# Merging the input projection and the gating stage of a hybrid decoder step, with two-part fp32r products

## The chip, the cores and the metric

The kernel runs on one core of one Trainium2 chip. The metric is the device time of one execution in microseconds (us), from the core's first instruction to its last plus a little around it. Three runs of the kernel before gave 2077.75 us in the median (2077.49 to 2078.82).

## The reference, cut to what matters

The reference is one step of a decoder layer for 1024 prompt tokens and 32 sample tokens (8 sequences of 4), 1056 in all, each with 1024 features. The part in question is its beginning:

```python
h = _rmsnorm(x, p['g_mix'])
u, v, q, kc, vc, ks, vs, kw, vw, gates = _split_in(h @ p['w_in'])   # 512, 512, 512, 6 x 128, 24 columns
...
u = gelu(u); v = _layernorm(gelu(v), ln_v_g, ln_v_b)                # _gmlp_mixer
mixed = einsum('gts,ncsgd->nctgd', w_s * causal, v) + b_s           # _sgu: 8 groups, chunks of 128 tokens
a_out = u * mixed
...
merged = concat([_rmsnorm(a_out, g_a), _rmsnorm(b_out, g_b)])       # _mix_out
x = x + merged @ w_o
```

Between `a_out` and `merged` stand the compression of keys and values, the attention of the samples and the attention of the prompt; after it come cross-attention and a gated feed-forward part. Everything is float32 at the interface.

## The kernel before

**Stages.** `program` runs the stages one after another, each a block in which the five engines have their own instruction streams and which all engines leave together: `input_phase`, `gating_phase`, `compress_phase`, `sample_attention`, `prompt_attention`, `mix_output`, then cross-attention and the feed-forward part. A tensor in SBUF is either feature-major (features on the 128 partitions, tokens along the row, `K.XT`, `K.HT`, `K.FM`) or token-major (128 tokens on the partitions, `K.U`, `K.V`, `K.VT`).

**input_phase** (L153). SP loads x in three pieces of 352 tokens. ACT squares each piece (L103), TensorE sums the squares over the features with a matrix of ones (L124, eight matmuls a piece), ACT takes the root (L133), VectorE inverts it and writes h = x * gain / rms into `K.HT` (L140, L147). Only then come the products: 8 chunks of 128 output features (q, and four of the key and value parts) times 3 pieces, each of 8 fp32 matmuls of 352 columns (L265), evacuated by ACT (L238). A ring of two buffers takes the weights. From the third chunk on, one piece of the bias rows is made behind each chunk (L274, 33x8 times up to 512 columns; L243). SP's queue also carries all other loads in program order: the token-major weights `w_tm`, two gathers of two sequences each (L295: 8 pages of 128 KB a sequence, whose numbers are read from the page table into registers), the operands of the gating, and at the end the writes of the bias rows, `fm` and the old window rows (`win_old`, from DRAM to DRAM).

**gating_phase** (L313). For each of 9 tiles of 128 tokens (the last has 32) TensorE makes u, v and the rest as 8 fp32 matmuls each of 512, 512 and 280 columns, with `K.HT` as the stationary operand and the weights as the moving one (L373). ACT applies gelu (L388, L389) and the sums for the layer norm, VectorE normalises v and copies the rest out. For each pair of tiles, 8 matmuls mix v over the tokens (L362), and VectorE adds the bias and multiplies by u (L418). SP loads the weights of the compression (`w_cmp1`, 1 MB each for k and v) when the last product is done.

**compress_phase** (L456). VectorE splits rows of `K.FM` (L498); SP moves them, then gathers the second half of the sequences, loads windows and gathers the selected pages (L295); TensorE runs six rounds (L573, L567, L586, L591). PE begins only when both halves of `w_cmp1` are there.

**mix_output** (L1056). The gated part is token-major: ACT squares it (L1124), VectorE scales it (L1159), TensorE turns each tile with four transposes (L1213), VectorE takes it out (L1164). The attention part is feature-major and goes through `FeatureNorm`. The product with `w_o` is 3 pieces x 8 chunks (L1230); turns of later tiles stand between the chunks.

**The feed-forward part** already splits operands: a number is held as high (rounded to fp32r by ACT) and low (the rest, by VectorE or POOL), and a product is three fp32r matmuls, high*high, high*low and low*high (L1622, L1640; the splits in L1722, L1731, L1784 and L1591).

Of the kernel before, what the change touches and what calls it, by code (L numbers as in the profile page):

```python
# [18 lines left out]
F32R = mybir.dt.float32r  # L19
I32 = mybir.dt.int32  # L20
ALU = mybir.AluOpType
# [131 lines left out]
def input_phase(nc, K, I, O):  # L153

    S = K.sem
    hold = K.top[:, O_VT:O_VT + 2 * KD * FREE3]
    sq = [hold[:, KD * FREE3 * u:KD * FREE3 * (u + 1)].rearrange("p (c n) -> p c n", c=KD) for u in range(2)]
    L = VECS + VECW
    oh = K.top[:BUCKETS + 1, O_M:O_M + L]
    vec = K.top[:H, O_M + L:O_M + 2 * L]  # L160
    root = [K.top[:, O_M + 2 * L + FREE3 * u:O_M + 2 * L + FREE3 * (u + 1)] for u in range(2)]
    ring = K.top[:, O_FM - 2 * KD * P:O_FM].rearrange("p (u k n) -> p u k n", u=2, k=KD)
    norm = FeatureNorm(nc, K, "mix", K.XT, K.gains[:, 0, :], PIECES, sq, root, K.bank[6], adds=0)
    const_came, eps_set, ones_set = S("const_came"), S("eps_set"), S("ones_set")
    x_came = [S(f"x_came{p}") for p in range(3)]
    w_came = [S(f"fm_w{u}") for u in range(2)]
    done, taken = S("fm_product"), S("fm_taken")
    came, rows, stored, product, set_ = S("bias_came"), S("bias_rows"), S("bias_dram"), S("bias_product"), S("bias_table")
    cuts = [(x, min(x + 512, L)) for x in range(0, L, 512)]
    tiles = [(c, p) for p in range(3) for c in range(2)] + [(c, p) for c in range(2, KD) for p in range(3)]  # L170
    nth = {tile: n for n, tile in enumerate(tiles)}

    with nc.Block() as block:
        @block.sync
        def _(sp):
            def weights(c):
                if c >= 2:
                    sp.wait_ge(done, nth[c - 2, 2] + 1)
                sp.dma_start(ring[:, c % 2], I["w_fm"][c]).then_inc(w_came[c % 2], 16)

            for p, (a, b) in enumerate(PIECES):
                sp.dma_start(K.XT[:, :, a:b], I["xt"][:, :, a:b]).then_inc(x_came[p], 16)
                if p == 0:
                    sp.dma_start(K.ident[:, :], I["ident"]).then_inc(const_came, 16)
                    sp.dma_start(K.gains[:, :, :], I["gains"]).then_inc(const_came, 16)
            weights(0)
            weights(1)
            sp.dma_start(oh, I["oh_v"]).then_inc(came, 16)
            sp.wait_ge(set_, 1)
            sp.dma_start(K.table[:BUCKETS, :], I["rel_bias"]).then_inc(came, 16)  # L190
            sp.dma_start(K.page_table[:, :], I["page_table"]).then_inc(came, 16)
            w = K.big[:, O_W:O_W + KD * TMW].rearrange("p (k n) -> p k n", k=KD)
            for k in range(KD):
                sp.dma_start(w[:, k, :], I["w_tm"][k]).then_inc(K.wtm_sem, 16)
            weights(2)
            sp.wait_ge(norm.scaled, 3)
            sp.wait_ge(came, 48)
            gather(sp, K, 0, "cmp", 0, 2)
            weights(3)
            gather(sp, K, 0, "cmp", 2, 2)  # L200
            for c in range(4, KD):
                weights(c)
                if c == 5:
                    for to, of in gating_operands(K, I):
                        sp.dma_start(to, of).then_inc(K.gating_sem, 16)
# [16 lines left out]
        def _(act):  # L222
            def square(p):
                act.wait_ge(x_came[p], 16)
                for h in range(2):
                    norm.square(act, p, h)
# [1941 lines left out]
```

## Time and profile before

| | |
|---|---|
| median of three runs | 2077.75 us |
| the profiled execution, its time | 2076.87 us |
| its span, first to last instruction | 2075.0 us |
| first product of the input stage starts | 30.09 us |
| first product of the gating stage starts | 157.58 us |
| first product of the compression starts | 336.12 us |
| sample attention starts (TensorE) | 408.48 us |
| product with `w_o` runs | 732.33 to 859.53 us |

PE is TensorE's matmuls, PEld its weight loads, DVE VectorE, ACT ScalarE, POOL GpSimd, SP the engine that issues most DMAs (SPq is its issuing). An fp32 matmul has two records in the trace, an fp32r matmul has one (the views call both f32), and records overlap, since matmuls are pipelined: the pace of a stream is its length divided by its matmuls, not the mean of a record. "[x <-y]" behind a row is the idle time before it and what ended it.

### The profile page before, as it was taken

The page shows a single profiled execution, that of the slowest core. Times are in us where ns is not written, and L with a number is a line of the kernel's source. Part 1 is how long each engine was busy: PE and PEld are TensorE (multiplying, and loading weights), DVE is VectorE, ACT ScalarE, POOL GpSimd, SP SyncE. Part 2 cuts the span into 40 slices and gives each one's busy share as a digit, 9 for nine tenths or more (in the row PEclk, how much of TensorE's full clock was granted, in tenths as well). Part 3 has the DMA queues.
Part 4 walks back from the last instruction along what each step waited for, and adds up shares of the span by engine and source line. Part 5 has one row for each costly group of instructions (what it writes and reads, how often), then busy time and mean ns, then how long its engine had stood idle before and what let it go on. Part 6 is the DMA issues. An engine that isn't in the chain of part 4 may idle for free. (4 is left out here: it accounts for less than half of the span.)

```text
span 2075.0 us, 26291 instructions
## 1 busy us (share of the span) xinstructions
PE 1935.3 (93%) x10926; PEld 1532.2 (74%) x10926; DVE 849.8 (41%) x1832; ACT 504.9 (24%) x1103; POOL 221.3 (11%) x98
## 2 busy tenths in 40 slices
PE   7999998948999789899978899999999999999997
PEld 4554555725767655656666466999999999999997
DVE  3001214047787545310032123545554555455547
ACT  2112221006888721000022022201111121112112
POOL 0000000000000000000000000313331333133320
PEclk9999999968999889999999999999999999999999
DMA  5512004741112120221033400201110111011102
GB/s 216 144 36 111 1 0 130 209 140 52 52 52 85 62 81 0 108 75 41 21 122 133 171 1 1 80 26 62 61 40 22 61 62 43 20 61 62 45 21 84
DMA packets 97002, 145.12 MB, mean 70 GB/s; under 512 B 40621, under 2 KB 73453, under 8 KB 94989
## 3 DMA queue, kind: packets, MB, share of 16 engines
q1 hardware_dynamic: 92798, 140.30, 19.8%
q10 hardware_dynamic: 4088, 3.17, 0.5%
q8 instruction: 86, 1.41, 0.3%
q14 instruction: 30, 0.25, 0.0%
HBM read 132.37 MB, written 14.19 MB: 71 GB/s over the span
## 5 line engine op out<-in xcount | busy, mean ns | idle before, releaser
L1622 PE MATMUL ps<-ff_in_high,ff_weights_low 128*128 128x352 f32 x1056 | 342.6, 324 | 0.0
L1622 PE MATMUL ps<-ff_in_high,ff_weights_high 128*128 128x352 f32 x1056 | 340.2, 322 | 0.0
L1622 PE MATMUL ps<-ff_in_low,ff_weights_high 128*128 128x352 f32 x1056 | 338.0, 320 | 0.0
L1622 PEld LDWEIGHTS ps<-ff_in_high,ff_weights_high 128*128 128x128 f32 x1056 | 198.8, 188 | 0.3
L1622 PEld LDWEIGHTS ps<-ff_in_low,ff_weights_high 128*128 128x128 f32 x1056 | 198.3, 188 | 0.2
L1622 PEld LDWEIGHTS ps<-ff_in_high,ff_weights_low 128*128 128x128 f32 x1056 | 198.1, 188 | 0.0
L1826 DVE TENSOR_TENSOR x<-ps,x 128x352 f32<-128x352 f32 x216 | 113.4, 525 | 134.5 <-PE ps L1640 134.5
L373 PE MATMUL ps<-big 128*128 128x512 f32 (+3 forms) x432 | 160.4, 533 | 6.2 <-DVE top L406 6.2
L1640 PE MATMUL ps<-ff_act_high,ff_down_high 128*128 128x352 f32 (+1 forms) x496 | 158.3, 319 | 0.2
L1640 PE MATMUL ps<-ff_act_high,ff_down_low 128*128 128x352 f32 (+1 forms) x496 | 156.5, 316 | 0.0
L1640 PE MATMUL ps<-ff_act_low,ff_down_high 128*128 128x352 f32 (+1 forms) x496 | 156.5, 315 | 0.0
L1591 POOL TENSOR_TENSOR ff_weights_low<-ff_weights,ff_weights_high 128x1024 fp32r<-128x1024 f32 x44 | 106.0, 2409 | 472.1 <-ACT ff_weights_high L1722 472.1
L373 PEld LDWEIGHTS ps<-big 128*128 128x128 f32 (+1 forms) x432 | 78.6, 183 | 86.9 <-issue 79.6
L1230 PE MATMUL ps<-big 128*128 128x352 f32 x384 | 118.9, 469 | 7.5 <-DVE big L1164 5.5
L1022 ACT ACTIVATE big<-big 128x63 f32<-128x63 f32 (+8 forms) x192 | 114.3, 608 | 21.5 <-DVE big L965 21.4
L1691 PE MATMUL ps<-big 128*128 128x352 f32 x384 | 115.6, 463 | 1.3 <-PEq L1432 1.3
L265 PE MATMUL ps<-big,top 128*128 128x352 f32 x384 | 115.1, 460 | 1.2 <-DMA top<-in_w_fm 1.2
L1276 PE MATMUL ps<-big,top 128*128 128x352 f32 x384 | 113.8, 459 | 0.0
L1230 PEld LDWEIGHTS ps<-big 128*128 128x128 f32 x384 | 73.9, 194 | 49.1 <-DVE big L1164 5.9
L265 PEld LDWEIGHTS ps<-big,top 128*128 128x128 f32 x384 | 72.5, 190 | 45.1 <-ACT top L238 3.4
L1691 PEld LDWEIGHTS ps<-big 128*128 128x128 f32 x384 | 73.7, 192 | 42.6 <-issue 2.7
L1276 PEld LDWEIGHTS ps<-big,top 128*128 128x128 f32 x384 | 73.0, 190 | 40.9 <-issue 0.5
(273 smaller groups left out, 2853.4 us busy)
## 6 DMA issues: line engine op xcount, KB each, us to landing
ff_weights<-in_w_up SPq DMA_DIRECT2D x22, 512.0 KB, 4.0
ff_weights<-in_w_gate SPq DMA_DIRECT2D x22, 512.0 KB, 4.3
ff_down<-in_w_down SPq DMA_DIRECT2D x22, 512.0 KB
x<-in_xt SPq DMA_DIRECT2D x6, 1408.0 KB, 9.7
top<-in_mem_kt SPq DMA_DIRECT2D x7, 1024.0 KB, 10.9
big<-in_w_tm SPq DMA_DIRECT2D x8, 652.0 KB, 16.2
top<-in_mem_v SPq DMA_DIRECT2D x5, 1024.0 KB, 17.4
top<-in_w_fm SPq DMA_DIRECT2D x8, 512.0 KB, 4.2
```

The costliest lines, as they stand in the source:

```text
L265: last = nc.tensor.matmul(K.bank[3 * (c % 2) + p][:, 0:b - a], ring[:, c % 2, k, :], K.HT[:, k, a:b], start=k == 0, stop=k == KD - 1)
L373: last = nc.tensor.matmul(K.bank[3 * (t % 2) + s][:r, 0:b - a], K.HT[:, k, t * P:t * P + r], w[:, k, a:b], start=k == 0, stop=k == KD - 1)
L1022: nc.scalar.activation(s[:, x:y], s[:, x:y], ACT.Exp, bias=m[:, b:b + 1], scale=-1.0, accum_out=m[:, 8 + b:9 + b]).then_inc(exps, 1)
L1230: last = nc.tensor.matmul(K.bank[n % 4][:, 0:b - a], w[:, c, k, :], K.HT[:, k, a:b], start=k == 0, stop=k == KD - 1)
L1276: last = nc.tensor.matmul(K.bank[QB[c % 2][p]][:, 0:b - a], xq_ring[:, c % 2, k, :], K.HT[:, k, a:b], start=k == 0, stop=k == KD - 1)
L1591: nc.gpsimd.tensor_tensor(w_low[:, s], landing[:, s], w_high[:, s], ALU.subtract).then_inc(low_done[s], 1)
L1622: last = nc.tensor.matmul(K.bank[3 * s + x][:, 0:b - a], wt[:, s, ws], h[:, k, a:b], start=k + n == 0, stop=k == KD - 1 and n == 2)
L1640: last = nc.tensor.matmul(bank[:, 0:b - a], wt[:, at], x[:, c % SLOTS, a:b], start=first and e + m == 0, stop=end and c == chunks[-1] and ...
L1691: last = nc.tensor.matmul(K.bank[(6, 7, 1, 4)[n % 4]][:, 0:b - a], w[:, c, k, :], K.HT[:, k, a:b], start=k == 0, stop=k == KD - 1)
L1826: nc.vector.tensor_tensor(K.XT[:, o, a:b], K.bank[6 + n % 2][:, 0:b - a], K.XT[:, o, a:b], ALU.add).then_inc(down_taken, 1)
```

## The change

One block, `mixer_inputs`, takes the place of `input_phase` and `gating_phase`:

- x is no longer normalised ahead of the products. ACT makes high(x * gain), VectorE low(x * gain); the products run on those, and 1/rms is multiplied in when a product is taken out of PSUM. For that `turn` makes 1/rms by tokens with nine one-column matmuls. The tokens come in groups of 384, 384 and 288, and the squares are added up on VectorE, so that the sum takes one matmul a group.
- v and the rest (280 columns) are made token-major, three tiles at a time, with three fp32r matmuls in place of one fp32 matmul; the low parts of these weights are made by VectorE. Everything else, u included, is made feature-major in 12 chunks x 3 pieces x 8 x 3 fp32r matmuls; ACT makes the high parts of the weights, POOL the low parts.
- The mixing writes feature-major: for each pair of groups 16 matmuls of 64 output rows each, the two groups on different halves of the output rows. `K.U` becomes feature-major.
- The bias rows are made behind chunks 1 and 2 and written out soon after. The gathers of the first half come after chunk 5, one sequence at a time, with one load of weights behind each. `win_old` is written behind them. One of the two `w_cmp1` loads waits for the block's last product.
- In `mix_output` the gated part goes through `FeatureNorm`; the 36 transposes and their scaling are gone. In `compress_phase` SP waits for the outputs.

The core of the diff:

```diff
-        input_phase(nc, K, I, O)
-        gating_phase(nc, K, I, O)
+        mixer_inputs(nc, K, I, O)
...
+            for kk in range(4):                        # SP
+                sp.dma_start(wv_landing[kk], I["w_v"][kk]).then_inc(wv_came[kk], 16)
+                sp.dma_start(K.XT[:, 2 * kk:2 * kk + 2, a:b], I["xt"][:, 2 * kk:2 * kk + 2, a:b]).then_inc(x_came[kk], 16)
...
+            sp.wait_ge(done, 18)
+            sp.wait_ge(mix_added, 5)
+            sp.wait_ge(mixed, 5)
+            sp.wait_ge(oh_came, 48)
+            sp.dma_start(K.cmp_w1[0], I["w_cmp1"][0]).then_inc(K.cmp_w1_came[0], 16)
+            for n in range(4):
+                gather(sp, K, 0, "cmp", n, 1)
+                weights(8 + n)
+            sp.wait_ge(sig, 2)
+            sp.dma_start(K.gates_dram, K.GT[:SROWS, 8, :]).then_inc(K.gates_sem, 16)
+            for v in range(2):
+                sp.dma_start(O["win_old"][v], I["win_old"][v][:, TS:WIN, :]).then_inc(K.out_sem, 16)
+            sp.wait_ge(done, 3 * CHUNKS)
+            sp.dma_start(K.cmp_w1[1], I["w_cmp1"][1]).then_inc(K.cmp_w1_came[1], 16)
+            sp.wait_ge(taken, 3 * CHUNKS)
+            sp.dma_start(O["fm"].rearrange("c p n -> p c n"), K.FM[:, 4:8, :]).then_inc(K.out_sem, 16)
...
+            for i in range(CHUNKS):                    # POOL
+                pool.wait_ge(f_high, i + 1)
+                nc.gpsimd.tensor_tensor(part(i, 1), landing(i), part(i, 0), ALU.subtract).then_inc(f_low, 1)
...
+            by_tokens(0, 0, {3: lambda: norm.spread(pe, 0)})          # PE
+            by_tokens(0, 1, {2: lambda: turn(0)})
+            by_tokens(1, 0, {1: lambda: norm.spread(pe, 1), 3: lambda: turn(1)})
+            by_tokens(1, 1, {0: lambda: norm.spread(pe, 2), 3: lambda: turn(2)})
+            by_tokens(2, 0, {})
+            by_tokens(2, 1, {})
+            for i in range(CHUNKS):
+                for p, (a, b) in enumerate(PIECES):
+                    if p == 0:
+                        pe.wait_ge(f_low, i + 1)
...
+                    for k in range(KD):
+                        for e, (wt, xs) in enumerate(((part(i, 0), high), (part(i, 0), low), (part(i, 1), high))):
+                            last = nc.tensor.matmul(K.bank[3 * (i % 2) + p][:, 0:b - a], wt[:, k, :], xs[:, k, a:b],
+                                                    start=k + e == 0, stop=k == KD - 1 and e == 2)
...
+                    if i in (1, 2):
+                        bias(3 * (i - 1) + p)
+                    if (i, p) in ((2, 2), (3, 0), (3, 1), (3, 2)):
+                        mix(3 * (i - 2) + p - 2)
+                    if (i, p) == (4, 0):
+                        mix_sample()
...
             gather(sp, K, 1, "cmp")                    # compress_phase, SP
+            sp.wait_ge(K.out_sem, 16 * K.outs(0))
...
+            def gated_piece(p):                        # mix_output, VectorE
+                gated.scale(dve, p, lambda c, a, b: K.HT[:, c, a:b])
+                    if p < 2 and c == 4:
+                        gated_piece(p + 1)
...
-                    if p < 2 and c in (1, 3, 5):       # mix_output, PE
-                        turn(3 * p + 3 + c // 2)
                     if p < 2 and c == 2:
+                        gated.spread(pe, p + 1)
```

In `by_tokens(g, s, between)` (s = 0 for v, 1 for the rest) PE runs, for each pair of feature blocks kk, the products high*high, high*low and low*high over 2 feature blocks and 3 tiles; it waits for the parts of the weights in group 0, for the parts of x in each group, and from group 1 on for the PSUM banks to be taken by ACT (v) or VectorE (the rest). What stands in `between` runs behind the named kk. On ACT `take_v(g)` does gelu and the sums of v; `weights(i)` makes a high part as soon as chunk i - 2 is done.

## Rows read from the trace of the kernel before

**Rows 1.** The profile page, busy time of each engine, share, instructions.

```profile
PE 1935.3 (93%) x10926; PEld 1532.2 (74%) x10926; DVE 849.8 (41%) x1832; ACT 504.9 (24%) x1103; POOL 221.3 (11%) x98
```

**Rows 2.** The chain that ended last, in order of time: start, us, what.

```profile
1179.14 0.04 issue
...
1388.43 46.13 PE ps L1622 x288
...
2015.81 13.45 PE ps L1640 x108
```

**Rows 3.** Timeline of PE, 0 to 345 us: start, us, line, tiles, count [idle].

```profile
10.35 7.15 PE L124 MATMUL ps<-top,ones 128*128 128x352 f32 x16 [10.35 <-ACT top L103]
...
19.58 4.97 PE L124 MATMUL ps<-top,ones 128*128 128x352 f32 x16 [2.08 <-ACT top L133]
...
120.09 1.02 PE L274 MATMUL ps<-top,table 33*8 33x512 f32 x2
...
157.58 54.71 PE L373 MATMUL ps<-big 128*128 128x512 f32 x144 [6.19 <-DVE top L406]
212.13 1.95 PE L362 MATMUL ps<-top 128*128 128x128 f32 x16
213.91 35.18 PE L373 MATMUL ps<-big 128*128 128x512 f32 x96
...
331.09 1.88 PE L362 MATMUL ps<-top 32*32 32x64 f32 x16 [6.29 <-DVE top L418]
336.12 15.48 PE L573 MATMUL ps<-x,big 128*128 128x256 f32 x64 [3.15 <-PEq L331]
```

**Rows 4.** Windows, 2 to 181 us: length, busy times, granted clock, DMA share, GB/s.

```profile
2.00:4.00 2.00, 0.00 (x0) 0.00 (x0) 0.00 (x0) 0.00 (x1) 0.00 (x0) 1.00 0.72 189
4.00:6.00 2.00, 0.00 (x0) 0.00 (x0) 0.00 (x0) 0.00 (x0) 0.00 (x0) 1.00 1.05 370
...
161.00:181.00 20.00, 20.00 (x55) 10.24 (x54) 0.51 (x2) 3.59 (x8) 0.00 (x0) 0.99 0.47 189
```

**Rows 5.** Groups by line and shape, 1179 to 2075 us, the last 0 to 345.

```profile
L1591 POOL TENSOR_TENSOR ff_weights_low<-ff_weights,ff_weights_high 128x1024 fp32r<-128x1024 f32 x44 | 106.0, 2409 | 472.1 <-ACT ff_weights_high L1722 472.1
...
L1722 ACT ACTIVATE ff_weights_high<-ff_weights 128x1024 fp32r<-128x1024 f32 x44 | 46.6, 1061 | 193.3 <-PE ps L1622 193.3
...
L1784 DVE SCALAR_TENSOR_TENSOR ff_in_low<-x,gains,ff_in_high 128x352 fp32r<-128x352 f32 x24 | 16.1, 678 | 13.6 <-ACT ff_in_high L1731 13.6
...
L140 DVE RECIPROCAL top<-top 128x352 f32<-128x352 f32 x3 | 7.1, 2350 | 19.5 <-ACT top L133 19.5
```

**Rows 6.** Timeline of PE, 403 to 420 us: matmuls on parts of the output rows.

```profile
403.68 0.65 PE L586 MATMUL ps<-big,x 128*64 128x252 f32 x4
...
417.01 3.15 PE L692 MATMUL ps<-x,big 128*32 128x512 f32 x16
```

**Rows 7.** DMA issues by line, KB each, median us to landing; SP's timeline of a gather.

```profile
top<-in_win_kt SPq DMA_DIRECT2D x1, 1024.0 KB, 5.7
...
x<-in_b2v SPq DMA_DIRECT2D x1, 64.0 KB, 22.0
...
55.76 13.47 SPq L295 DMA_DIRECT2D x<-in_pool_cmp  x16
```

**Rows 8.** Timelines of SP and DVE at the end of the compression, 377 to 409 us.

```profile
377.58 29.86 SPq L295 DMA_DIRECT2D x<-in_pool_sel  x32
...
405.69 0.68 DVE L522 TENSOR_TENSOR top<-ps,x 63x512 f32<-63x512 f32 x1 [0.84 <-PE ps L591]
408.14 0.29 DVE L738 TENSOR_TENSOR big<-top 128x128 f32<-128x128 f32 x1 [1.76 <-PEq L480]
```

**Rows 9.** Timeline of PE in mix_output, 732 to 860 us.

```profile
732.33 12.72 PE L1230 MATMUL ps<-big 128*128 128x352 f32 x32 [5.49 <-DVE big L1164]
744.88 0.60 PE L1213 MATMUL ps<-ident,top 128*128 128x128 f32 x4
...
798.27 0.66 PE L1213 MATMUL ps<-ident,top 128*128 128x128 f32 x4 [2.42 <-DVE top L1159]
```

More of the change, by code:

```diff
@@ new lines, in mixer_inputs, with landing, part, tiles_of @@
+    cuts = [(a, min(a + 512, L)) for a in range(0, L, 512)]
+    def landing(i):
+        a = x[:, 1024 * (i % 2):1024 * (i % 2) + 1024] if i < 6 else fm[:, T * (6 + i % 2):T * (6 + i % 2) + 1024]
+        return a.rearrange("p (k n) -> p k n", k=KD)
+    def part(i, which):
+        return (early if i < 6 else late)[:, which, i % 2]
+    def tiles_of(g):
+        return range(3 * g, 3 * g + 3)
+    def columns(g):
+        return [(P, 3 * g, 3 * g + 3)] if g < 2 else [(P, 6, 8), (SROWS, 8, 9)]
@@ L342, in _ @@
             sp.dma_start(O["vt_s"], K.VT[:SROWS, 8, :]).then_inc(K.out_sem, 16)
+            sp.wait_ge(v_ready, 3)
+            sp.dma_start(O["gmlp_v"], K.V[:SROWS, TILES - 1, :]).then_inc(K.out_sem, 16)
+            weights(4)
+            sp.wait_ge(rows, len(cuts))
+            sp.dma_start(K.vec_dram, vec).then_inc(stored, 16)
+            weights(5)
+            sp.wait_ge(done, 3)
+            weights(6)
+            weights(7)
+            sp.wait_ge(done, 18)
+            sp.wait_ge(mix_added, 5)
@@ new lines, in turn, with bias @@
+            def turn(g):
+                if g == 0:
+                    pe.wait_ge(small_came, 16)
+                pe.wait_ge(norm.rstd, g + 1)
+                for t in tiles_of(g):
+                    last = nc.tensor.matmul(K.bank[7][:rows_of(t), t:t + 1], rstd[:, t * P:t * P + rows_of(t)], K.ident[:, 0:1],
+                                            start=True, stop=True)
+                last.then_inc(turned, 1)
+            def bias(b):
+                if b == 0:
+                    pe.wait_ge(oh_came, 48)
+                    pe.wait_ge(norm.std, 3)
+                    pe.wait_ge(rtok_made, 3)
+                if b >= 2:
+                    pe.wait_ge(rows, b - 1)
+                y, z = cuts[b]
+                nc.tensor.matmul(K.bank[6 + b % 2][:H, 0:z - y], K.table[:, :], oh[:, y:z], start=True, stop=True).then_inc(product, 1)
@@ new lines, in _ @@
+            act.wait_ge(eps_set, 1)
+            norm.square(act, 0, 0)
+            norm.square(act, 0, 1)
+            for c in range(KD):
+                x_part(1, c)
+            norm.root(act, 0)
+            norm.square(act, 1, 0)
+            norm.square(act, 1, 1)
+            act.wait_ge(K.gating_sem, 16 * len(gating_operands(K, I)))
+            take_v(0)
+            for c in range(KD):
+                x_part(2, c)
+            norm.root(act, 1)
+            norm.square(act, 2, 0)
```

603 lines of the change are left out of this document (328 added, 275 removed).

## The prediction

> **What bounds the kernel now.** I read the page first. PE is busy 93% of the span and no other engine half of it [rows 1], so the question in each stage is what PE does there and what it waits for. The chain of waits names PE alone, but it can be followed back only to 1179.14 us [rows 2]; the stages that change lie ahead of that, and for those I read PE's own timeline [rows 3]. It shows three things. Until 10.35 us PE does nothing, and until the first product at 30.09 us (the table above) it only adds squares for the norm, waiting for ACT in between. From there products follow one another, up to a gap of 6.19 us where the gating block begins, and again until the last mixing matmuls at 331.09 + 1.88 = 332.97 us (6.29 us of idle ahead of them). The compression's first matmul starts at 336.12 us. So the first 336 us are PE work with 30 us of head and 6.19 + 6.29 + 3.15 = 15.6 us of gaps and tail. An earlier end of that work moves everything behind it, if nothing there hangs on a load that does not move along.
>
> **Prices of a matmul.** The feed-forward part runs the three-part fp32r product that the change uses: 288 matmuls of 352 columns in 46.13 us, 0.1602 us each, and near the end 108 of 264 columns in 13.45 us, 0.1245 each [rows 2]. 
>
> The Trainium skill (TensorE: Matmul & The Clock Gate, Back-to-back issue gap) gives columns / 2.4 GHz plus about 2.5 ns for an isolated gap. The rows at 352 and 264 columns lie 11 to 12 ns above that, so the rows decide. By the rule the token-major products below would take 216 x (0.2158 + 0.1192) = 72.4 us.
>
> **The new block, along PE.** I laid the five instruction streams side by side, each instruction behind the one before it on its engine and behind its waits.
>
> *Start.* The first products need a quarter of v's weights (0.52 MB), the first two feature blocks of x (0.39 MB) and one high part of each. Loads begin at about 2 us and move 189, then 370 GB/s [rows 4]: both are there at about 6 us. ACT's high part of 1024 columns takes 1.06 us [rows 5] and begins when the weights land, near 5 us; for x's 384 columns I take 0.6. First matmul at **6.7 us**. TensorE's first matmuls are slow: the first 16 records of L124 took 7.15 us, the next 16 took 4.97 [rows 3], so I add **2.2**.
>
> *Token-major products.* 3 groups x 3 tiles x 8 blocks x 3 parts = 216 matmuls of 512 columns and 216 of 280: 216 x (0.2268 + 0.1312) = **77.3 us**.
>
> *Feature-major products.* 12 chunks x 3 pieces x 24 = 864 matmuls x 0.1602 = **138.4 us**.
>
> *Small ones.* Sums of squares: three matmuls near 4.97 / 8 = 0.62, **1.8** (before: 24 of them). 1/rms by tokens: nine of one column; no row has such a stream, I take 0.17 each, **1.5** (0.3 to 2.5). Bias rows: six as before, at about 1.0 with the last one half [rows 3], **5.4**.
>
> *Mixing.* 64 matmuls of 128 columns instead of 32. One after the other they cost what L362 shows, (213.91 - 212.13) / 8 = 0.2225 [rows 3], 14.2 us. But neighbours write different halves of the output rows, and such matmuls overlap: 8 of 512 columns on quarters take 3.15 us where four cycles a column would make 6.8, and two of 252 columns on halves take 0.65 where that makes 0.84 [rows 6]. The pair is the nearest row and holds the end of its last matmul, which a stream hides; I take 0.145 each, **9.3** (7 to 14.2). The samples' eight, of 32 columns: **0.8** (the eight of 64 columns took 1.88 behind a gap [rows 3]).
>
> *Stalls.* What my schedule leaves: 1.6 us at the second group of v, where the banks wait for ACT's gelu, which waits for 1/rms by tokens (squares, root, an inversion of 2.35 us or more [rows 5], `turn`); 0.6 ahead of the first mixing, for the last bias row. **2.2** in all. The cover is thin in the first 70 us, since ACT and VectorE make all parts of x and of the early weights there: per quarter of the first group at most 3.3 us of VectorE (x's low part twice, 0.68 us for 352 columns [rows 5], and the weights' low part, by its 1024 columns at most 2.0) against 18 x 0.2268 = 4.1 of PE. With every instruction of ACT and VectorE 1.2 times as long the schedule ends 3.6 us later, 1.3 times 7.6; with loads at 250 GB/s in place of 370, 6.8.
>
> *Behind SP's waits.* POOL's low part takes 2.41 us [rows 5] and ACT's high part 1.06, against 11.5 us a chunk: covered. Behind chunk 5 SP issues 1 MB, then four times a gather of 8 pages and a weight load. Sixteen pages take 13.47 us to issue [rows 7], with the read of the page numbers about 8.2 for eight. Chunk 8's weights then land about 13 us behind chunk 5, their low part is there at 17, PE wants it at 23; later chunks have more. Covered, at no cost; without the cover rival C has the price. `win_old` starts about 32 us ahead of the end and needs some 20 (189 GB/s over the 20 us in which it ran before [rows 4]).
>
> The waits that are new: SP's for chunk 5 and the mixing holds back the gathers and four weight loads, just priced. ACT's for the mixing and three outputs, ahead of chunk 6's high part, holds back the later high parts; the outputs are issued some 70 us earlier. VectorE's for the stored bias rows stands at chunk 4, two chunks behind the last of them; it would hold back the taking of banks. SP's for all outputs in the compression stands behind 32 gathers, nearly 30 us behind the 2 MB of `fm`; the windows and the pages are behind it. I take nothing for each.
>
> Sum: 6.7 + 2.2 + 77.3 + 138.4 + 1.8 + 1.5 + 5.4 + 9.3 + 0.8 + 2.2 = **245.6 us** for the last product, against 332.97.
>
> **Into the compression.** Its first matmul now waits for 1 MB of `w_cmp1` that SP issues when the last product is done: a load of 1 MB took 5.7 us to land [rows 7], so PE starts at 245.6 + 6.0 = 251.6 instead of 336.12: **84.5 us earlier** (the step from product to compression grows from 3.15 to 6.0; bounds 5 to 10, the write of `fm` runs beside it). SP's own chain there (moves, gather, windows, pages) starts when the block starts, about 4 us ahead of PE. Before, SP ended the block, at 377.58 + 29.86 = 407.44, a little behind VectorE at 406.37 [rows 8]; then PE ends it: **1.1 us** more.
>
> **mix_output.** Removed from PE: six groups of transposes inside the product, 0.43 us each beyond the overlap (2.6), and most of the 2.42 us of waiting for L1159 [rows 9]. Added: two sums at 0.6, and VectorE's inversion (2.35) and four products (2.1) at piece 1, chunk 4, which push the heads' scaling and make PE wait some 0.6 longer at piece 2. The start shortens by 0.4 of the 5.49 us. Net **1.9 us** gained, between 4.5 gained and 3 lost.
>
> Behind it nothing changes. Total: 84.5 + 1.1 + 1.9 = 87.5. The profiled execution took 2076.87 us, 0.9 below the median: 1989.4, or 1990.3 in medians. I forecast **1990 us**.
>
> **The rivals.**
>
> *A. ACT and VectorE set the pace of the first 70 us.* For it: two group changes where PE waits on a chain of four engines, and the inversions between them. Against it: VectorE has at most 3.3 us of work per 4.1 of PE. 12 us more: 2002.
>
> *B. The compression waits for its weights.* `w_cmp1`'s second half stands behind `win_old` on the same queue; a small load issued behind `win_old` took 22.0 us to land before [rows 7]. If the gathers run late by more than about 12 us, each further microsecond is one of waiting, up to 20. Against it: those 12 us. 10 us more: 2000.
>
> *C. Weights stuck behind gathers.* If a gather with its weight load takes over 12.3 us, the wait of chunk 11 grows by 4 us for each further one; at 20 us it is 31: 2021. Against it: 8.2.
>
> *D. The token-major products pay no addition.* With other operands in the two roles the weight load is hidden wholly: 216 x (0.0135 + 0.0145) = 6.0 us less, 1984. Against it: 264 and 352 columns show the same addition. The Trainium skill's rule above would leave 2.5 ns of it.
>
> **How the numbers follow.** The forecast 0.72, A 0.12, B 0.06, C 0.04, D 0.03, E 0.02; 0.01 for a loss that eats the gain. The bounds of the unknown costs: token-major products -6.0 to +1.3, mixing -2.3 to +4.9, stalls -2.2 to +10, the load +4, mix_output -2.6 to +4.9. The low ends add up to 1977, and I take 1979; the high ends don't all meet, and with A and B inside I take 2012. Within 0.2% (4 us, about what a measurement of this kernel can tell from no change): 0.01. Slower: 0.03, for E and worse. Faster: 0.96.
>
> **What would show it.** The first fp32r matmul near 7 us; the end of the 216 + 216 near 90 us; each chunk at 11.5 us, at full clock; the mixing at 2.3 us per pair of groups; no gap of PE above 2 us ahead of the last product near 246; the compression starting 6 us later, sample attention near 324; from there the same distances, but for 2 us in mix_output. Wrong would be the sum if gaps stand at the group changes (A), ahead of chunks 8 to 11 (C) or ahead of the compression (B), or if a 512-column matmul is not near 0.227 us (D, E).

## The result, and the profile after

The changed kernel takes 1997.35 us (median of four runs) against 2077.62 for the kernel before: a ratio of 0.9614, 95% interval 0.9599 to 0.9629. The forecast was 1990, between 1979 and 2012. The profiled execution of the kernel after took 1999.25 us, its span 1997.4; a second profile of the same kernel (the first experiment below) took 1996.0.

The page of the kernel after, busy time of each engine:

```profile
PE 1869.9 (94%) x11416; PEld 1577.5 (79%) x11416; DVE 891.0 (45%) x1855; ACT 505.8 (25%) x1079; POOL 250.0 (13%) x110
```

PE has 65 us less of work than in [rows 1] and is still the engine that bounds the kernel. Its timeline in the new block and behind it answers to [rows 3]:

```profile
8.10 2.90 PE L360 MATMUL ps<-mix_w_v,mix_x_high 128*128 128x512 f32 x6 [8.10 <-ACT mix_x_high L443]
10.80 2.76 PE L360 MATMUL ps<-mix_w_v,mix_x_low 128*128 128x512 f32 x6
13.36 3.26 PE L360 MATMUL ps<-mix_w_v,mix_x_high 128*128 128x512 f32 x12
...
20.66 1.56 PE L360 MATMUL ps<-mix_w_v,mix_x_low 128*128 128x512 f32 x6
22.06 2.96 PE L360 MATMUL ps<-mix_w_v,mix_x_high 128*128 128x512 f32 x12
...
29.07 0.93 PE L360 MATMUL ps<-mix_w_rest,mix_x_low 128*128 128x280 f32 x6
29.84 1.70 PE L360 MATMUL ps<-mix_w_rest,mix_x_high 128*128 128x280 f32 x12
...
39.79 1.65 PE L360 MATMUL ps<-mix_w_v,mix_x_high 128*128 128x512 f32 x6 [1.40 <-ACT top L455]
...
248.25 0.32 PE L427 MATMUL ps<-mix_x_high,mix_w_late 128*128 128x352 f32 x1
255.32 16.22 PE L772 MATMUL ps<-x,top 128*128 128x256 f32 x64 [6.75 <-DMA big<-in_w_cmp]
...
295.48 14.08 PE L772 MATMUL ps<-big,top 128*128 128x256 f32 x64 [0.25 <-DMA big<-in_pool_cmp]
...
329.29 5.78 PE L875 MATMUL ps<-big 128*128 128x512 f32 x8 [3.45 <-DVE big L937]
```

The block runs from 8.10 to 248.57 us with two gaps, 1.40 us at 39.79 and 0.5 ahead of the mixing. Six matmuls of 512 columns take 22.06 - 20.66 = 1.40 us (0.2333 each), six of 280 take 0.77 (0.1283 each); but the first twelve take 13.36 - 8.10 = 5.26 us, nearly twice that. A window of PE over them (length, busy, granted clock, DMA share, which is the mean busy share of the core's 16 DMA engines, and GB/s) shows the full clock all the same:

```profile
8.10:13.30 5.20, 5.20 (x12) 1.00 1.04 406
```

Behind the block the profile shows what was not forecast. Here is SP's own timeline there, first of the kernel before, then of the kernel after:

```profile
337.99 5.07 SPq L487 DMA_DIRECT2D big<-big  x8
344.63 28.21 SPq L295 DMA_DIRECT2D big<-in_pool_cmp  x32
```

```profile
248.60 0.37 SPq L327 DMA_DIRECT2D big<-in_w_cmp  x1
249.16 0.39 SPq L329 DMA_DIRECT2D out_fm<-top  x1
252.18 8.91 SPq L685 DMA_DIRECT2D big<-big  x8
262.69 30.16 SPq L170 DMA_DIRECT2D big<-in_pool_cmp  x32
...
298.12 30.14 SPq L170 DMA_DIRECT2D x<-in_pool_sel  x32
```

The eight moves inside SBUF take 8.91 us where they took 5.07, right behind the 2.1 MB write of `fm`, and SP's last gather ends at 298.12 + 30.14 = 328.26 us (these are times of issuing). VectorE is done before that (end of the compression, then start of the next block):

```profile
325.88 0.68 DVE L721 TENSOR_TENSOR top<-ps,x 63x512 f32<-63x512 f32 x1 [0.84 <-PE ps L790]
328.95 0.29 DVE L937 TENSOR_TENSOR big<-x 128x128 f32<-128x128 f32 x1 [2.38 <-PEq L678]
```

So in this profile SP still ends the compression, as in [rows 8], by 328.26 - 326.56 = 1.7 us.

How far the kernel after is ahead of the kernel before, at the first matmul of each stage (from the first and last start that the trace gives for each line; the last column is the forecast's):

| point | before | after | lead | lead, second profile | forecast |
|---|---|---|---|---|---|
| last product or mixing done | 332.97 | 248.57 | 84.4 | 84.3 | 87.4 |
| compression's first | 336.12 | 255.32 | 80.8 | 80.8 | 84.5 |
| sample attention's first | 408.48 | 329.29 | 79.2 | 81.4 | 85.6 |
| memory's keys, first | 859.5 | 777.7 | 81.8 | 85.0 | 87.5 |
| cross attention's queries, first | 925.2 | 844.2 | 81.0 | 84.2 | 87.5 |
| feed-forward, first | 1295.2 | 1215.3 | 79.9 | 83.1 | 87.5 |
| last ten sums, end | 2066.3 | 1988.4 | 77.9 | 81.1 | 87.5 |

About 3 us are missing at the end of the block, 0.7 more at the compression's start, and the rest behind it. The experiments ask which of these is a mechanism and which is scatter.

### The profile page after: what moved, and what is told of

It is laid out like the page before. It is cut to its first block and busy times, and to the rows that moved or that the text cites. A ratio compares the mean times of both kernels' runs of the same rounds, so it can differ in the third digit from the quotient of the medians.

```text
span 1997.4 us, 27321 instructions
## 1 busy us (share of the span) xinstructions
PE 1869.9 (94%) x11416; PEld 1577.5 (79%) x11416; DVE 891.0 (45%) x1855; ACT 505.8 (25%) x1079; POOL 250.0 (13%) x110
## 5 line engine op out<-in xcount | busy, mean ns | idle before, releaser
L1434 PE MATMUL ps<-big,top 128*128 128x352 f32 x384 | 113.8, 459 | 0.0
L1434 PEld LDWEIGHTS ps<-big,top 128*128 128x128 f32 x384 | 73.0, 190 | 40.9 <-issue 0.5
L1880 ACT ACTIVATE ff_weights_high<-ff_weights 128x1024 fp32r<-128x1024 f32 x44 | 46.6, 1062 | 193.3 <-PE ps L1780 193.3
L1798 PEld LDWEIGHTS ps<-ff_act_high,ff_down_high 128*128 128x128 f32 x496 | 93.1, 188 | 0.7 <-DVE x L2031 0.6
L1798 PEld LDWEIGHTS ps<-ff_act_high,ff_down_low 128*128 128x128 f32 x496 | 93.2, 188 | 0.1
L1798 PEld LDWEIGHTS ps<-ff_act_low,ff_down_high 128*128 128x128 f32 x496 | 93.0, 188 | 0.0
```

The costliest lines, as they stand in the source:

```text
L1434: last = nc.tensor.matmul(K.bank[QB[c % 2][p]][:, 0:b - a], xq_ring[:, c % 2, k, :], K.HT[:, k, a:b], start=k == 0, stop=k == KD - 1)
L1798: last = nc.tensor.matmul(bank[:, 0:b - a], wt[:, at], x[:, c % SLOTS, a:b], start=first and e + m == 0, stop=end and c == chunks[-1] and ...
L1880: nc.scalar.activation(w_high[:, s], landing[:, s], ACT.Copy).then_inc(w_split[s], 1)
```

## The experiments

Ratios are against the kernel before. A difference between two variants under about 3 us is not told apart by the times here; there the traces decide.

### The same kernel again

No edit.

> The changed kernel, unchanged, profiled a second time. Theory one (what the profile lost behind the compression, from a lead of 79.2 us at the sample attention to 77.6 us at the end, is how the runs scatter): the lead at the sample attention's first matmul (329.29 us in the first profile) comes again within 0.5 us, and the lead at the end comes out different, up to 81 us. Theory two (the loss belongs to the change): the last ten sums again take 4.75 us where the kernel before took 2.48 us, and the span is again 1997.4 us within 0.5.

Measured: 1997.03 us, ratio 0.9611 [0.9595, 0.9627]; profiled 1996.0. The block is the same to 0.1 us. The difference arises at one place, where the sample attention's first eight matmuls start (SP's and PE's timelines, second profile):

```profile
296.54 29.19 SPq L170 DMA_DIRECT2D x<-in_pool_sel  x32
```

```profile
255.36 16.30 PE L772 MATMUL ps<-x,top 128*128 128x256 f32 x64 [6.77 <-DMA big<-in_w_cmp]
...
327.04 3.06 PE L875 MATMUL ps<-big 128*128 128x512 f32 x8 [1.39 <-DVE big L937]
```

SP ended its gather 2.5 us earlier, at 296.54 + 29.19 = 325.73 us, now ahead of VectorE (326.37), and the same matmuls took 3.06 us instead of 5.78. Windows of PE around them (length, busy, granted clock, DMA share, GB/s), first of the first profile, then of the second:

```profile
325.00:329.00 4.00, 0.85 (x15) 0.87 0.58 168
329.00:335.00 6.00, 5.71 (x8) 0.52 0.86 264
```

```profile
327.00:330.00 3.00, 2.96 (x8) 1.00 0.74 171
```

With a longer idle stretch ahead (3.45 against 1.39 us) TensorE starts at the lower of its two levels, 1.2 GHz, with a shorter one at 2.4. So a wait costs more than its length. The kernel before paid this as well: behind 2.83 us of idle its same eight matmuls took 5.84 us, at a granted clock of 0.52. Against it the first profile lost nothing here by the clock; the second gained what no term of the forecast had. The lead behind it, 3.1 to 3.2 us better, stays to the end. My first theory said that the late losses are scatter; half of it holds. The lead at the sample attention, which it expected within 0.5 us, moved by 2.2. The end differs, but for the reason just shown, and the loss from 81.8 to 77.9 (85.0 to 81.1) comes back the same in both: 0.8 us around the load of `w_mk` (a wait of 8.5 us against 7.1), 1.1 between the queries and the feed-forward, and 2.0 in the last ten sums. Those took 4.1 us in both, at a granted clock of 0.50, and in the next experiment 2.0, at 1.00. The idle stretch ahead of them is 2.94 us (once 2.93) in all; three of the twelve profiles with the new block show the quick form, nine a slower one. I count that part as scatter, though with a single profile of the kernel before, a quick one, that is not proven.

### Feature rows written early

```diff
+            for n in range(3):
+                sp.wait_ge(taken, 27 + 3 * n)
+                sp.dma_start(O["fm"][n], K.FM[:, 4 + n, :]).then_inc(K.out_sem, 16)
             sp.wait_ge(done, 3 * CHUNKS)
...
-            sp.dma_start(O["fm"].rearrange("c p n -> p c n"), K.FM[:, 4:8, :]).then_inc(K.out_sem, 16)
...  (compression, behind the gather)
             sp.wait_ge(K.out_sem, 16 * K.outs(0))
+            sp.dma_start(O["fm"][3], K.FM[:, 7, :]).then_inc(K.out_sem, 16)
```

> The write of the four feature rows (2.1 MB), which the changed kernel issues at 249.16 us, right ahead of the eight moves inside SBUF, goes out row by row as chunks 8 to 10 are taken, the last row behind the page gathers. Theory (SP's queue ends the compression, and the moves take 8.91 us instead of 5.07 because they share the transfers' engines with the write): the eight moves take 5 to 6 us, SP's last gather there ends 3 to 4 us earlier, at 324 to 325 us, but TensorE, which still starts at 255.3 us, now ends the compression at 326.6 us; the sample attention's first matmul comes at about 327.6 us instead of 329.29, and the time falls by 1.7 us. Rival (the moves are slow for another reason, the write has no part in it): the moves still take 8 to 9 us and the sample attention starts at 329.3 us.

Measured: 1994.09 us, 0.9599 [0.958, 0.9619]; not told apart from the kernel after. SP's timeline in the compression:

```profile
249.92 5.79 SPq L687 DMA_DIRECT2D big<-big  x8
...
288.18 5.89 SPq L815 DMA_DIRECT2D top<-in_win_v  x4
295.24 30.51 SPq L170 DMA_DIRECT2D x<-in_pool_sel  x32
```

The moves take 5.79 us: the write beside them was what stretched them. But the part gained is lost again: the windows' loads, now behind the last row's write, take 5.89 us instead of 3.38, and SP ends at 325.75 while TensorE is done at 322.0. The sample attention starts at 326.79 us, where the block had ended 1.8 us earlier by a quicker start (below). SP alone sets the end here, where the theory had TensorE.

### TensorE does not wait for the second weight

```diff
-            for v in range(2):
-                pe.wait_ge(came_w[v], 16)
+            pe.wait_ge(came_w[0], 16)
             for n in range(len(rounds)):
+                if n == 1:
+                    pe.wait_ge(came_w[1], 16)
                 hidden_rows(n)
```

> TensorE waits for the second compression weight only ahead of the second round, which is the first to use it. Theory (SP's queue ends the compression, TensorE's 6.75 us wait is hidden): the first compression matmul comes at about 250.5 to 251.5 us instead of 255.32, but the round on the second half's pages waits for them until 295.5 us as before, and the sample attention still starts at 329.3 us within 0.4; the time stays. Rival (the wait of 6.75 us is where the missing gain of the prediction went): the sample attention starts at about 325 us and the time falls by 4 us.

Measured: 1998.86 us, 0.9619 [0.9603, 0.9635]: no gain, as the theory said, though not by its chain. PE's timeline, and PE's windows with the granted clock:

```profile
248.87 14.05 PE L772 MATMUL ps<-x,top 128*128 128x256 f32 x64 [1.64 <-PEq L267]
...
295.83 16.95 PE L772 MATMUL ps<-big,top 128*128 128x256 f32 x64 [8.99 <-DMA big<-in_pool_cmp]
```

```profile
286.60:295.80 9.20, 0.24 (x4) 0.76 0.98 253
295.80:299.00 3.20, 3.17 (x8) 0.50 1.09 339
```

TensorE starts early and then waits 8.99 us for the pages. Behind that gap the clock is at the lower level, the round takes 16.95 us instead of 14.08, and the sample attention starts at 330.46 us, later than the 329.3 expected; the times do not tell it apart. TensorE, done at 329.1 us, ends the compression here; SP's last gather ends at 325.9. The early start did save something: the first round takes 14.05 us here, against 16.22 behind the wait of 6.75 us.

### Both edits

> Both edits of the two runs beside it: the feature rows written early, and TensorE's wait for the second compression weight put off to the second round. Theory (two chains of nearly one length end the compression, SP's and TensorE's, so that each edit alone shows at most a part): the sample attention's first matmul comes at 324.5 to 325.5 us, 4 to 5 us earlier than the 329.29 of the changed kernel, and the time falls by 4 to 5 us. Rival (only TensorE's wait matters): the same as with the wait put off alone. Rival (neither matters): 329.3 us.

Measured: 1996.89 us, 0.961 [0.9594, 0.9626]. The theory of two chains fell in this form. PE's timeline:

```profile
293.51 15.88 PE L776 MATMUL ps<-big,top 128*128 128x256 f32 x64 [7.54 <-DMA big<-in_pool_cmp]
...
327.06 3.06 PE L880 MATMUL ps<-big 128*128 128x512 f32 x8 [1.39 <-DVE big L942]
```

The pages still come at 293.5 us. SP issues their gather behind the moves, which wait for VectorE: 257.3 to 286.8 us. The other 6.7 us lie between the end of the issuing and the landing, while the last row's write and the windows' loads are under way (DMA share 0.94 to 1.02 from 288 to 294 us); how much of them those transfers cost is not shown. TensorE's early start only widens its gap. What both edits leave untouched is the place of the moves in SP's queue.

### Moves on ScalarE's queue

```diff
-            sp.wait_ge(dei, 2)
-            for v in range(2): ... sp.dma_start(own[v]..., dein[v]...)
             gather(sp, K, 1, "cmp")
...  (ScalarE)
+            act.wait_ge(dei, 2)
+            for v in range(2): ... act.dma_start(own[v]..., dein[v]...)
```

with TensorE's wait put off as above.

> Two edits in the compression: the eight moves inside SBUF go out from ScalarE's queue instead of SP's, so that SP's gather of the second half's pages no longer stands behind them, and TensorE waits for the second compression weight only ahead of the round that uses it. Theory (SP's queue and TensorE's start are two chains of nearly one length): the gather begins at about 250 us instead of 262.7 and its pages are there at 282, ahead of TensorE, which starts at 249 us and comes to them at 287; the compression ends without a wait at 317 to 318 us, the sample attention's first matmul comes at 318.5 to 320 us instead of 327.0 to 329.3, and the time falls by 8 to 10 us, to about 1988. Rival (the gather's 30 us are set by the transfers beside it, 2.1 MB of feature rows and 1 MB of weights, not by its place in the queue): its pages come at 290 us or later, and the sample attention starts at 322 us or later.

Measured: 1997.11 us, 0.961 [0.9592, 0.9627]: what the rival expected came about. SP's timeline and PE's:

```profile
251.48 37.15 SPq L170 DMA_DIRECT2D big<-in_pool_cmp  x32
```

```profile
294.51 16.39 PE L772 MATMUL ps<-big,top 128*128 128x256 f32 x64 [7.23 <-DMA big<-in_pool_cmp]
```

The gather starts 11 us earlier and takes 37.15 us instead of 30: out of the moves' way in the queue, it runs beside the write, the weight load and the moves themselves. Which of them stretches it, the next run asks.

### All three edits

> Three edits at once: the feature rows written early, the eight moves on ScalarE's queue, TensorE's wait for the second compression weight put off. Theory (what stretched the gather to 37.15 us when only the moves had left SP's queue is the 2.1 MB write beside it): the gather takes 29 to 31 us again, its pages are there at 282 to 284, TensorE comes to them at 285 to 287 without a wait, and the sample attention's first matmul comes at 317 to 320 us; the time is 1985 to 1989. Rival (the moves on the other queue stretched it): the pages come at 288 us or later, the sample attention at 324 to 328, the time 1992 to 1996.

Measured: 1988.9 us, 0.9579 [0.9566, 0.9592]. SP's timeline and PE's:

```profile
250.29 31.91 SPq L170 DMA_DIRECT2D big<-in_pool_cmp  x32
...
283.39 5.85 SPq L816 DMA_DIRECT2D top<-in_win_v  x4
290.43 30.11 SPq L170 DMA_DIRECT2D x<-in_pool_sel  x32
```

```profile
287.06 14.08 PE L776 MATMUL ps<-big,top 128*128 128x256 f32 x64
...
321.58 5.62 PE L880 MATMUL ps<-big 128*128 128x512 f32 x8 [4.15 <-DVE big L942]
```

The gather, still out of the moves' way, is back at 31.91 us with the write moved off, so the write was what stretched it. Now TensorE comes to the pages without a wait (no bracket at 287.06). The time is in the theory's range; the sample attention starts at 321.58 us, 1.6 us later than its range, because SP, held 5.85 us by the windows, ends at 320.5 while TensorE is done at 317.4. So the write of `fm` and the order in SP's queue were each a part, and neither showed a gain without the other: with the write moved away, the gather stood behind the moves; with the moves taken out of SP's queue, the gather was stretched by the write. All these runs have TensorE's wait put off; what the two are worth without that is not shown.

### fp32 instead of three fp32r matmuls

```diff
-        sb = lambda ...: mem.enter_context(nc.sbuf_tensor(name, shape, F32R, side=side))
+        sb = lambda ...: mem.enter_context(nc.sbuf_tensor(name, shape, F32, side=side))
...
+                            if e:
+                                continue
...
-                        for e, (wt, xs) in enumerate(((part(i, 0), high), (part(i, 0), low), (part(i, 1), high))):
+                        for e, (wt, xs) in enumerate(((part(i, 0), high),)):
```

> The products of the new block in fp32 again: the high parts are whole fp32 copies, and one matmul in place of three; the low parts are still made, but not multiplied. Everything else stays. Theory (the block is TensorE work almost throughout, so a matmul's price goes into the time in full): 72 pairs of 512 and 280 columns at fp32's price (a tile of three banks took 35.18 / 2 = 17.6 us before) make 96.4 us in place of 78, and 288 products of 352 columns at 0.603 us make 173.7 in place of 138.3; the last product comes at 302 us in place of 248.6, and the time rises by about 54 us, to 2051. Then 54 of the change's 80 us are fp32r's, the other 26 the joined block's. Rival (ScalarE, VectorE or the loads set the pace in the first 100 us): the token-major part ends at the same 94.5 us as with fp32r, and the time rises by at most 35 us.

Measured: 2051.85 us, 0.9865 [0.9845, 0.9886]: 54.8 us more than the kernel after (1997.03), at 54 expected. PE's timeline at the start:

```profile
7.75 23.38 PE L362 MATMUL ps<-mix_w_v,mix_x_high 128*128 128x512 f32 x48 [7.75 <-ACT mix_x_high L445]
```

The token-major part ends at 116 us instead of 94.5, the last product starts at 302.2 (302 expected), and the 54 us are there at the sample attention (383.2 against 329.3). TensorE's price goes into the time in full; some 54 of the 80 us are fp32r's, the other 25 are left for the joined block, as a difference: no run has the two old blocks with fp32r.

### Four gathers in one piece

```diff
+            gather(sp, K, 0, "cmp", 0, 4)
             for n in range(4):
-                gather(sp, K, 0, "cmp", n, 1)
                 weights(8 + n)
```

> The first half's four gathers go out in one piece ahead of the weights of chunks 8 to 11, instead of one ahead of each. Theory (the prediction's rival C, whose condition did not come about: weights stand behind gathers on SP's queue): the four gathers hold SP from 181 to about 211 us, chunk 8's weights land at 214 and their low part is there at about 217 us, where TensorE wants it at 202: a wait of 12 to 18 us once, the last product at about 264 us, and the time rises by as much, to about 2012. Rival (the weights do not depend on that order, or a later chunk has the time back): no wait, 1997 us.

Measured: 2015.17 us, 0.9696 [0.9675, 0.9717]. SP's timeline and PE's:

```profile
180.65 30.56 SPq L170 DMA_DIRECT2D x<-in_pool_cmp  x32
211.42 10.04 SPq L273 DMA_DIRECT2D top<-in_w_fm  x4
```

```profile
218.84 0.66 PE L427 MATMUL ps<-mix_x_high,mix_w_late 128*128 128x352 f32 x1 [16.90 <-POOL mix_w_late L340]
```

One wait of 16.90 us (12 to 18 expected), the last product at 267.6 us (264 expected), and the time rises by 18: nothing gives it back. The order "one gather, one weight" is worth that much.

### Low parts on GpSimd

```diff
+            for kk in range(4):
+                pool.wait_ge(wv_high, kk + 1)
+                nc.gpsimd.tensor_tensor(wv[:, 1, ...], wv_landing[kk], wv[:, 0, ...], ALU.subtract).then_inc(wv_low, 1)
...  (VectorE)
-                dve.wait_ge(wv_high, kk + 1)
-                nc.vector.tensor_tensor(wv[:, 1, ...], wv_landing[kk], wv[:, 0, ...], ALU.subtract).then_inc(wv_low, 1)
```

and the same for the two low parts of `w_rest`.

> The low parts of the early weights (of v and of the rest) on GpSimd instead of VectorE. Theory (the first group of products is bound by TensorE, and the low parts have slack): GpSimd takes some 2.4 us for 1024 columns where VectorE took 1.22; the first is there at about 10.5 us and wanted at 11.9 to 13.4, the later ones have more; the token-major part ends within 0.5 us of 94.4 (or of 92.6, where TensorE's first matmuls are slow for a shorter time), and the time stays. Rival (the two engines disturb one another, or GpSimd's low parts come late): TensorE waits in the first 30 us, and the token-major part ends 2 to 6 us later.

Measured: 1999.4 us, 0.9613 [0.9591, 0.9636]; the time alone tells nothing. The trace does, and my theory fell: TensorE waits three times, 2.9 us in all, and the feature-major part starts at 97.0 us with a first matmul at 7.7, against 92.7 to 94.0 in six other kernels with the same code up to there that start at 7.7 to 7.9. VectorE's and GpSimd's timelines, and VectorE's low parts in the kernel after (groups by line: busy, mean ns of one):

```profile
7.72 16.02 DVE L534 SCALAR_TENSOR_TENSOR mix_x_low<-x,gains,mix_x_high 128x384 fp32r<-128x384 f32 x6 [7.72 <-ACT mix_x_high L451]
...
23.66 1.14 DVE L534 SCALAR_TENSOR_TENSOR mix_x_low<-x,gains,mix_x_high 128x384 fp32r<-128x384 f32 x2
```

```profile
7.18 10.38 POOL L340 TENSOR_TENSOR mix_w_v<-top,mix_w_v 128x1024 fp32r<-128x1024 f32 x4 [6.19 <-ACT mix_w_v L482]
17.52 5.79 POOL L344 TENSOR_TENSOR mix_w_rest<-top,mix_w_rest 128x1120 fp32r<-128x1120 f32 x2
```

```profile
L526 DVE SCALAR_TENSOR_TENSOR mix_x_low<-x,gains,mix_x_high 128x384 fp32r<-128x384 f32 x13 | 7.4, 614 | 8.1 <-ACT mix_x_high L443 8.1
```

Beside GpSimd's subtractions VectorE's first six low parts of x take 16.02 / 6 = 2.7 us each instead of 0.61, about the length of one GpSimd instruction (10.38 / 4 = 2.6, then 5.79 / 2 = 2.9). The two behind the end of GpSimd's work, at 17.52 + 5.79 = 23.31 us, take 1.14 us together. The Trainium skill (SBUF — State Buffer, SBUF: two separate sides) says that the two engines share one pair of ports as a lock that is held for a whole instruction, so that the other stands still; this goes for a VectorE instruction with two inputs from SBUF beside a GpSimd instruction that reads SBUF. The trace agrees: each VectorE instruction is stretched to about the length of GpSimd's, while GpSimd's 2.6 us are near the 2.41 of [rows 5]. So making these low parts on VectorE, as the change does, is worth some 3 us of TensorE's time, and I had given it nothing.

### A prepared start

```diff
             pe.wait_ge(ones_set, 1)
+            for _ in range(12):
+                nc.tensor.matmul(K.bank[7][:, 0:P], K.ones[:, :], K.ones[:, :], start=True, stop=True)
...  (ScalarE)
+            act.wait_ge(eps_set, 1)
+            nc.scalar.activation(K.stat[:, 1, 0:1], K.eps[:, :], ACT.Copy)
             act.wait_ge(const_came, 16)
```

> Two edits at the start: ScalarE loads its function table before the first weights land (a copy of one column ahead of the first wait; it took 1.28 us behind them), and TensorE multiplies the ones by themselves twelve times (128 columns, results not used) while it waits. Theory (the first matmul comes late by the table, and the first ones cost 0.46 instead of 0.23 us because TensorE had done nothing before them): the first product at 6.3 to 6.8 us instead of 7.7 to 8.1, the first twelve take 2.8 us instead of 4.3 to 5.7, the token-major part ends at 90 to 91 us instead of 92.6 to 94.4, and the time falls by 2.5 to 4 us. Rival (the slow price belongs to the first 10 to 13 us of an execution, whatever TensorE did before): the first twelve still take 4.3 us or more, and only the 1.3 us of the table are gained.

Measured: 1991.81 us, 0.9589 [0.9576, 0.9602]. PE's timeline:

```profile
1.01 5.49 PE L412 MATMUL ps<-ones 128*128 128x128 f32 x24 [1.01 <-POOL ones L336]
6.66 1.62 PE L360 MATMUL ps<-mix_w_v,mix_x_high 128*128 128x512 f32 x6 [0.16 <-ACT mix_x_high L445]
...
9.52 2.96 PE L360 MATMUL ps<-mix_w_v,mix_x_high 128*128 128x512 f32 x12
```

The first product comes at 6.66 us, the first twelve take 9.52 - 6.66 = 2.86 us, and the last product comes 2 to 4 us earlier than without, as expected; the medians lie 5.2 us apart, with intervals that leave room for less. The slow price belongs to a TensorE that has been idle, not to the first microseconds of an execution: at 6.66 us it is gone, where the kernel after still paid it until 13.36.

### All five edits

> All five edits: those of the two kernels beside it. Theory (the start's gain moves the whole block, and the compression's gain adds to it): the last product at about 244 us, the sample attention's first matmul 2.5 to 4 us ahead of that with the three edits alone, at 314 to 317 us, the time 1981 to 1986. Rival (the gains hide one another): no faster than the better of the two.

Measured: 1985.47 us, 0.956 [0.9547, 0.9574]: faster than both kernels and than the prepared start alone. Its median lies 3.4 us below that of the three edits, with intervals that overlap a little; there the trace decides. PE's timeline:

```profile
283.89 14.08 PE L780 MATMUL ps<-big,top 128*128 128x256 f32 x64
...
315.64 3.06 PE L884 MATMUL ps<-big 128*128 128x512 f32 x8 [1.39 <-DVE big L946]
```

TensorE comes to the pages without a wait, and the sample attention starts 13.7 us ahead of the first profile of the kernel after, at the full clock. That is 5.9 us ahead of the three edits alone, more than the 2.5 to 4 expected: the block ends 3.2 us earlier, and SP's windows take 3.60 us here instead of 5.85, so that SP no longer ends the compression.

## Why the prediction was right, and where it was off

The sign and the size held: 80 us gained of the 87 forecast, by the mechanism named, the price of TensorE's work. Step by step:

- *Products.* 864 feature-major matmuls at 0.160 us: as taken from [rows 2]. The token-major ones cost 216 x (0.2333 + 0.1283) = 78.1 us against 77.3. The 512-column price lies at the upper bound that was named (0.233), not at columns plus 0.0135; why it is 0.0200 above its columns, and 280 columns only 0.0116, stays open. Rival D asked for 0.2133 at 512 columns and fell. The Trainium skill (TensorE: Matmul & The Clock Gate, Back-to-back issue gap) gives 0.2133 + 0.0025 for an isolated gap; the trace shows 0.2333 in this stream, in which each matmul has its own weights. Rival E (four cycles a column) fell with the same rows.
- *Start.* First matmul at 8.10 us, not 6.7: ACT's function table, 1.28 us, was loaded only when the first weights had landed, and the sum had no term for it (ACT's timeline):

```profile
5.10 1.28 ACT L474 ACT_TABLE_LOAD   x1 [5.10 <-DMA top<-in_w_v]
```

  The slow first matmuls cost 5.26 - 12 x 0.2333 = 2.5 us, 0.3 over the 2.2 taken; profiles of other kernels with the same start show 1.3 to 2.5. The prepared start gave both back, which confirms the two terms.
- *Mixing, bias, sums, stalls.* From the last token-major to the last feature-major product 154.1 us pass, of which 138.2 are products; the other 15.9 answer to 5.4 + 9.3 + 0.8 + 0.6 = 16.1 in the sum. The 1.40 us at v's second group were forecast as 1.6.
- *Rivals A and C.* But for the two gaps of 1.40 and 0.5 us, both forecast, ACT and VectorE were ahead throughout, and each gather with its weight took 6.9 to 8.7 us of SP, under the 12.3 from which C decides. C's mechanism is real: put the gathers in one piece, and it costs 16.9 us. A's cover is thinner than I said: with GpSimd in VectorE's way it tears.
- *Into the compression.* 6.75 us for the step, against 6.0. Rival B did not come about as told (`win_old` was done: nothing is transferred from 236 to 248.6 us), but the wait stands in the profile. Taken away alone it gains nothing, since SP's pages come later still. The clock is lower behind it as well: the first round takes 16.22 us (granted clock 0.86; 16.30 us in the second profile), against 15.48 (0.91) behind the 3.15 us of the kernel before and 14.05 behind 1.64. The sum had no term for that.
- *The compression's end: a step that failed.* "Then PE ends it: 1.1 us more" and "I take nothing for each", the latter said also of SP's wait behind the write of `fm`. I had looked at what waits for the write, not at what is transferred beside it. It stretched the moves by 3.2 to 3.8 us and, through them, all of SP's chain; 1.6 us were lost in the first profile and 0.6 gained in the second, around SP's and TensorE's chains that end within 2 us of each other. In the second profile TensorE's chain does end it, as forecast; the 0.5 us that are missing there are within the 0.8 by which the first round is longer. The late end of the first profile also costs the lower clock, 2.7 us against the second, but the kernel before paid that too.
- *mix_output.* Forecast 1.9. The lead grows by 2.3 to 2.4 us between the prompt attention's first matmul and the memory's keys in both profiles, but 0.8 are given back one step later, in a longer wait for `w_mk`: "behind it nothing changes" was wrong there, since that load does not move along in full.
- *The rest.* 1.1 us between the queries and the feed-forward, and 2.0 in the last ten sums, at the clock of the moment; the second I count as scatter, the first is not settled.

In sum, by the second profile: 3.7 us up to the compression (start 1.3, slow matmuls 0.3, price 0.8, the wait 0.8, the rest of the block 0.5), 0.5 in the compression, 0.8 of `w_mk`, 3.1 late, less 1.7 that the lead grew more than forecast between (1.2 of it in the sample attention, behind the quicker first matmuls, which was luck and no term of the sum); 6.4 of the 6.6 us between 1989.4 and 1996.0.

## What to carry to other kernels

When a block gets shorter, read what its last instructions put on the queues: a write that cost nothing while the engine was busy now runs beside the next block's first moves. Where two chains end a stage within 2 us of each other, as here, an edit to one of them may show nothing by itself, and a wait made longer upstream can cost the clock behind it as well; price both chains and edit them together. An idle head (a function table that could be loaded, an engine that could be kept at work) is a cheap place to look in a kernel that is bound by one engine: four lines gave 2 to 4 us here by the traces and 5 by the medians (0.9611 to 0.9589, with intervals that overlap a little).

## What had not been expected of the hardware

- Twelve matmuls of 512 columns took 5.26 us behind an idle start (0.44 each, near 512 columns at 1.2 GHz = 0.427, though the granted clock of that window reads 1.00) and 2.86 behind twelve dummy products of 128 columns.
- An idle stretch of 2.83, 3.45, 4.15 or 8.99 us ahead of a stretch of matmuls left it at the lower clock (granted 0.52 and 0.50 where windows were read; 5.84, 5.78 and 5.62 against 3.06 us for the same eight); one of 1.39 us did not, and behind 2.94 us both came about in different runs.
- VectorE's low part of 384 columns, made from two SBUF tensors, went from 0.61 to 2.7 us beside GpSimd's subtractions of 1024 and 1120 columns (2.6 and 2.9 us each).
- A gather of 32 pages took 28.2 to 31.9 us to issue everywhere else in these profiles, and 37.15 where 3.1 MB were written and loaded beside its start.
